# Low parts on VectorE, results read ahead of the weight sums, and the first down-weight sums moved one pair on

## What is computed

```
D_FF = -(-8 * D_MODEL // (3 * 256)) * 256
...
    h = h + m @ w_o
    hn = rms_norm(h, norm2_g)
    gate, up = jnp.split(hn @ w_gate_up, 2, axis=-1)
    return h + (jax.nn.silu(gate) * up) @ w_down
```

## Time and profile before

| | |
|---|---|
| three runs | 2266.13, 2267.99, 2269.9 us; median 2267.99 |
| profiled execution | 2270.73 us, span 2269.0 us |
| TensorE busy | 2179.5 us, 96% |
| VectorE, ScalarE, POOL busy | 1428.4 us (63%), 913.6 us (40%), 1024.8 us (45%) |
| mean granted clock of TensorE | 0.985 |
| the MLP's up and gate blocks | 1142.9 to 1592.7 us |

### The profile page before, as it was taken

The page is one execution under the profiler, slowest core; times in us unless marked ns, Lnnn a source line. Parts: engine busy times, 40 slices in busy tenths (PEclk is TensorE's granted clock), DMA queues, the critical chain, the costliest instruction groups (busy, mean ns, idle before and its releaser), DMA issues.

```text
span 2269.0 us, 29879 instructions
## 1 busy us (share of the span) xinstructions
PE 2179.5 (96%) x10752; PEld 1800.1 (79%) x10752; DVE 1428.4 (63%) x2788; ACT 913.6 (40%) x1625; POOL 1024.8 (45%) x580
## 2 busy tenths in 40 slices
PE   6999999999999989999979999999999999999998
PEld 5886688998888777778857888888888878888886
DVE  4248799999932366655597666565557746206944
ACT  5234522233224574433442323323445554226743
POOL 1265433455544233225556545556588723121063
PEclk8999999999999999999999999999999999999999
DMA  5112111111224213025623545444876321111131
GB/s 189 45 49 73 56 47 51 51 52 38 66 83 140 64 48 98 29 93 177 199 66 126 176 144 177 144 169 171 293 250 201 115 105 54 47 47 38 39 121 74
DMA packets 243829, 238.46 MB, mean 105 GB/s; under 512 B 10337, under 2 KB 186110, under 8 KB 243694
## 3 DMA queue, kind: packets, MB, share of 16 engines
q1 hardware_dynamic: 239536, 223.49, 30.4%
q10 hardware_dynamic: 4158, 13.16, 1.4%
HBM read 174.54 MB, written 61.15 MB: 104 GB/s over the span
## 4 chain that ended last, share of the span: by engine, by line
PE 76%; DVE 7%; issue 2%; ACT 2%; POOL 1%; ACTq 0%; DVEq 0%
PE ps L982 23%; PE ps L1269 17%; PE ps L1297 9%; PE ps L1343 9%; PE ps L1159 6%; PE ps L1564 4%; PE ps L1542 2%; PE ps L1191 1%; DVE logit L2402 1%; PE ps L1134 1%; PE ps L1177 1%; PE ps L1527 1%; DVE pt_lo L2421 1%; PE ps L1511 1%; PE ps L1501 0%
## 5 line engine op out<-in xcount | busy, mean ns | idle before, releaser
L3030 POOL TENSOR_TENSOR w_lo<-w_raw,w_hi 128x1024 fp32r<-128x1024 f32 (+1 forms) x129 | 295.2, 2289 | 760.6 <-ACT w_hi L1593 760.6
L982 PE MATMUL ps<-x_hi,w_hi 128*128 128x512 f32 (+2 forms) x960 | 360.9, 376 | 4.0 <-DVE c_rs L2319 3.3
L982 PE MATMUL ps<-x_lo,w_hi 128*128 128x512 f32 (+2 forms) x960 | 359.1, 374 | 0.0
L982 PE MATMUL ps<-x_hi,w_lo 128*128 128x512 f32 (+2 forms) x960 | 357.1, 372 | 0.0
L982 PEld LDWEIGHTS ps<-x_hi,w_hi 128*128 128x128 f32 x960 | 180.9, 188 | 39.7 <-issue 9.1
L982 PEld LDWEIGHTS ps<-x_hi,w_lo 128*128 128x128 f32 x960 | 181.2, 189 | 28.7
L982 PEld LDWEIGHTS ps<-x_lo,w_hi 128*128 128x128 f32 x960 | 180.7, 188 | 28.6 <-issue 0.2
L2377 DVE MATCH_REPLACE8 score<-best,score 128x400 f32<-128x400 f32 (+3 forms) x224 | 185.2, 829 | 0.0
L2373 DVE MAX8 best<-score 128x8 f32<-128x400 f32 (+3 forms) x224 | 181.2, 842 | 1.4
L1593 ACT CAST w_hi<-w_raw 128x1024 fp32r<-128x1024 f32 (+1 forms) x129 | 127.7, 990 | 103.0 <-PE ps L982 73.0
L1269 PE MATMUL ps<-x_hi,wr_hi 128*128 128x512 f32 x352 | 139.5, 396 | 3.1 <-DVE x_lo L2526 2.0
(11 more groups left out here) (473 smaller groups left out, 5453.3 us busy)
## 6 DMA issues: line engine op xcount, KB each, us to landing
w_raw<-in_w_in SPq DMA_DIRECT2D x74, 512.0 KB, 3.7
wdr<-as_scratch SPq DMA_DIRECT2D x77, 256.0 KB, 4.0
rawg<-in_w_gate_up SPq DMA_DIRECT2D x22, 512.0 KB, 3.9
rawu<-in_w_gate_up SPq DMA_DIRECT2D x22, 512.0 KB, 5.4
wdr<-in_w_down SPq DMA_DIRECT2D x22, 512.0 KB, 6.4
as_scratch<-ac SPq DMA_DIRECT2D x44, 256.0 KB, 3.7
wt_scratch<-wdr SPq DMA_DIRECT2D x33, 256.0 KB, 4.9
as_scratch<-a SPq DMA_DIRECT2D x33, 256.0 KB, 4.0
```

The source lines that it names most:

```text
L982: mm = pe.matmul(ps[:, b, 0:n], w[:, s, P * k:P * k + P], r[:, k, t0:t0 + n], start=k == 0 and i == 0, stop=k == kd - 1 and i == 2 and ext ...
L3030: pool.tensor_tensor(w_lo[:, p % 2, 0:n], w_raw[:, p % 2, 0:n], w_hi[:, p % 2, 0:n], ALU.subtract).then_inc(wlo_done, 1)
```

## The change

Four things change. VectorE makes all low parts of y = 16 to 27, the even ones too, which POOL made. The three first result reads of pair 0 come right behind them; `block_low(13)` follows, then the other reads of pairs 0 and 1, and only then `combined_weights(2)` and `block_low(15)`. ScalarE no longer waits for `combined_weights(n)` before it casts P1 and P2 of a pair n from 2 on (they are loaded weights). And POOL's `down_combined(0)` and `down_combined(1)` move from (2, 0) and (2, 6) of its loop over pairs and steps to (3, 0) and (3, 4).

```diff
--- before.py
+++ after.py
@@ -1867,7 +1867,7 @@
                 else:
                     n, prod = product_of(q)
                     act.wait_ge(raw_pair[n % 2], RAW_PAIR_0[n % 2] + 32 * (n // 2 + 1))
-                    if n >= 2 or prod not in ("P1", "P2"):
+                    if prod not in ("P1", "P2"):
                         act.wait_ge(tw_done, TW_DONE_0 + 4 * n + 4)
                 if q >= SLOTS:
                     act.wait_ge(blk_done, BLK_DONE_0 + q - SLOTS + 1)
@@ -2519,11 +2519,11 @@
                 dve.tensor_tensor(sr(1, s), wdr[:, s % 4, :], sr(0, s), ALU.subtract).then_inc(sl_even, 1)
 
             def x_low(y):
-                if y % 2 == 0:
-                    return
                 dve.wait_ge(xh_done, y + 1)
+                if y == 16:
+                    dve.wait_ge(*low_x(14))
                 prod, k = FIRST[y // 4], y % 4
-                dve.tensor_tensor(xb(1, prod, k), x_source(y), xb(0, prod, k), ALU.subtract).then_inc(xl_odd, 1)
+                dve.tensor_tensor(xb(1, prod, k), x_source(y), xb(0, prod, k), ALU.subtract).then_inc(xl_odd if y % 2 else xl_even, 1)
 
             def inverse(h):
                 c = slice(4 * h, 4 * h + 4)
@@ -2603,22 +2603,20 @@
                 dve.wait_ge(*low_x(8 + k))
                 dve.tensor_tensor(mix[:, 4 + k, half(1)], mix[:, 4 + k, half(1)], mix[:, k, half(1)], ALU.add).then_inc(s0_done, 1)
             block_low(9)
-            x_low(17)
-            x_low(19)
+            for k in range(16, 20):
+                x_low(k)
             for k in range(4):
                 dve.wait_ge(s0_done, S0_DONE_0 + 4 + k + 1)
                 dve.tensor_tensor(mix[:, k, half(1)], mix[:, 4 + k, half(1)], mix[:, k, half(0)], ALU.subtract).then_inc(s0_done, 1)
             block_low(11)
-            x_low(21)
-            x_low(23)
+            for k in range(20, 24):
+                x_low(k)
             for k in range(4):
                 dve.wait_ge(s0_done, S0_DONE_0 + 8 + k + 1)
                 dve.wait_ge(*low_x(4 + k))
                 dve.tensor_tensor(mix[:, 4 + k, half(0)], mix[:, 4 + k, half(0)], mix[:, k, half(1)], ALU.subtract).then_inc(s0_done, 1)
-            x_low(25)
-            x_low(27)
-            block_low(13)
-            combined_weights(2)
+            for k in range(24, 28):
+                x_low(k)
             for n in range(2):
                 a = a_st[0][n]
                 dve.wait_ge(r1_done, n + 1)
@@ -2629,9 +2627,11 @@
                 dve.tensor_tensor(g1[n][:, :], a[0][:, :], ps[:, bank_of(n, "P7"), :], ALU.add).then_inc(po_done, 1)
                 dve.wait_ge(po_done, po(n, 2))
                 dve.tensor_tensor(a[1][:, :], g1[n][:, :], ps[:, bank_of(n, "P5"), :], ALU.add).then_inc(po_done, 1)
+                if n == 0:
+                    block_low(13)
                 dve.tensor_tensor(g1[n][:, :], g1[n][:, :], ps[:, bank_of(n, "P4"), :], ALU.add).then_inc(po_done, 1)
-                if n == 0:
-                    block_low(15)
+            combined_weights(2)
+            block_low(15)
             for n in range(2):
                 a = a_st[0][n]
                 dve.wait_ge(blk_done, BLK_DONE_0 + 13 + n)
@@ -3231,13 +3231,7 @@
             x_low(12)
             x_low(14)
             block_low(10)
-            x_low(16)
-            x_low(18)
-            x_low(20)
-            x_low(22)
             block_low(12)
-            x_low(24)
-            x_low(26)
             block_low(14)
             block_low(16)
             for n in range(2):
@@ -3265,9 +3259,9 @@
                     block_low(7 * n + 6 + i)
                     if n == FC - 1 and i >= 1:
                         inner_low(i - 1)
-                    if (n, i) in ((2, 0), (2, 6)):
+                    if (n, i) in ((3, 0), (3, 4)):
                         pool.wait_ge(am_done, AM_DONE_0 + 4)
-                        down_combined(i // 6)
+                        down_combined(i // 4)
                     if i == 3 and n % 2 == 0 and n >= 4:
                         down_combined(n // 2)
                     if i == 5:
```

## The result

The changed kernel takes 2278.71 us (median of 5 runs, 2276.58 to 2285.77), the kernel before 2267.99 (5 runs, 2263.74 to 2270.45). The ratio is 1.0052, with a 95% interval from 1.004 to 1.0064: slower by some 11.8 us. The forecast was 7.4 us, with a range up to 2279.5; the ratio applied to the median of before gives 2279.8, just outside, though the median of its own five runs lies inside. The profiled execution of the changed kernel took 2280.36 us, its span is 2278.6.

A forecast was written before the change was run, and what follows sets the result against it. The prediction took TensorE, busy 96% of the span, as the bound, so only its idle time or clock matters. It summed -6.3 + 10.9 + 2.8 = +7.4 us on 2268.0, giving 2275.4 us, range 2269.5 to 2279.5.

The forecast's parts named there:

- the price of ScalarE's wait: Later pairs' P1 and P2: POOL's low part may hold VectorE 1.2 us in the weight sums; costed at nothing.
- The true wait of q12: 6.6 us stall at q12: waits for VectorE's queue (read of P5), not `wr_lo`; q12 would start 6.2 us earlier.
- one hold of 1.2: VectorE's queue before q12: POOL's q12 weights (1.2 us) fall among four low parts.
- 6.3 us earlier at q20: Pair 2's P3: q20 starts at 1212.1 instead of 1218.42; bounds 5.0 and 7.5 us.
- a slow clock at q12: Slow clock after q12's stall would be hidden by q20, since q18 and q20 wait for VectorE.
- 10.9 us later from q20 to q25: Moved sums delay SP's load of pair 4: q20's start to q25's takes 25.4 us, before 14.46; bounds 23.2 and 27.
- 2.8 us for the clock: After the stall before q25, TensorE works at its lower level and loses 2.8 us; bounds 1.7 and 3.5.
- cover of 1.5 us: Odd pairs: from L2701's end (starts 1270.00, takes 0.68) to P2's end at 1272.2, called the closest.
- a new short wait in each pair of odd number: Sign of being wrong: pairs of odd number show a new short TensorE wait each.
- The faster rival: Before q25: pair 4's load is not what is waited for; kernel takes 2261.1 us if the chain fits entirely; chance 0.08.
- waits of 1.5 to 2.5 us at q18 and q20: Sign of being right: q18 and q20 each wait 1.5 to 2.5 us for VectorE.

The follow-up runs named there:

- the best version: Kernel before plus new VectorE/POOL order, sums at (2, 4) and (3, 4), pair 4's load first, q12's low weights on VectorE, ScalarE's wait dropped for pair 2: 2262.23 us, ratio 0.9965.

## Why the prediction was right, and where it was not

The step that failed is the price of ScalarE's wait, put at nothing; the other terms came out within 1.1 us each.

- **The true wait of q12** (VectorE's read of P5, not the `wr_lo` in the row): right. With the reads ahead of the weight sums q12 started 7.3 us earlier. The forecast had 6.2: it put POOL's q12 weights into VectorE's queue as one hold of 1.2. In fact VectorE was not held at all, its four low parts took 2.49, and POOL stood. That extra 1.1 was gone again at `combined_weights(2)`, which waited 1.2 us for the load of pair 2, a wait that the forecast did not have.
- **6.3 us earlier at q20**: 5.2. L2707 ended 69.1 us after q0, just as forecast, but by luck: q18 started 1.3 us later than forecast, mainly since a weight sum was held (L2505, 1.64 us for 0.69), and the inner sums behind it took one hold instead of two. The forecast hid a slow clock at q12 behind later waits and had none at q18. L2707 ended at 1209.1, before q19 did, so the stretch of 3.3 us at the lower level behind q18's stall lay on the path of q20 and cost what was left.
- **10.9 us later from q20 to q25**: 10.6, each link within 0.3 us of its row. Three experiments show the cause: moving the sums alone makes a loss of 9.3 us, and moving them back or issuing the load first makes the changed kernel 10 to 11 us faster.
- **2.8 us for the clock**: 2.9. That it fits so well is luck: behind stalls of 10.2, 10.5 and 11.1 us at the same place in three other runs (ScalarE's wait back, the sums moved alone, q12's weights alone) the lower level lasted 4.9, 4.2 and 3.4 us, not 5.7.
- **ScalarE's wait, "so I cost it at nothing": the step that failed.** The mechanism was written down (POOL's low part falls into `combined_weights`), but its cover of 1.5 us was read from pair 5 and called the closest. In the kernel before, pair 9 has less. The read on VectorE, and the ScalarE operation that starts as P2 ends:

```profile
1348.68 0.68 DVE L2701 TENSOR_TENSOR a<-r1a,ps 128x512 f32<-128x512 f32 x1
```

```profile
1350.28 0.60 ACT L1900 ACTIVATE g0a<-ps 128x512 f32<-128x512 f32 x1 [0.81 <-PE ps L1269]
```

  From the end of the one to the start of the other is a cover of 0.9, less than the 1.1 that a hold costs. Pair 15 has 0.9 too and pair 19 has 1.2; pairs 7, 11, 13 and 17 have 1.7 to 2.0. All are some 0.3 too large if taken this way, since P7 starts 0.2 us before that ScalarE operation, and 0.15 us after a read that it waits for.

  What it cost: in the changed kernel TensorE stalls before P7 of pairs 9, 13, 15 and 19, 1.9 us by the profile's idle time. By the starts of the blocks (2.79 us for one that nothing stops) the blocks around these four places and one in pair 17 take 3.2 us more, and the clock behind q25 takes 2.7; that makes the +5.8 of the table. One hold is not the whole of it: in pair 13 the weight sums also start 1.0 us later against P7 than before, behind POOL's queue. The other runs agree. From q25 to the last block it takes 362.1 us in the two kernels without ScalarE's wait and without a long stall there, and 359.5 in the four that have the wait and no long stall. Giving the wait back took 3.4 us off the ratio, though with overlapping intervals. So this is most of the gap between +7.4 and +11.8. The prediction had named it as a sign of being wrong, a new short wait in each pair of odd number; it came in four of them.
- The edits one at a time, each on the kernel before, gave +9.3 (the sums), -1.8 (the new order, an interval that reaches no change) and +1.6 (the wait, not to be told from nothing). They sum to +9.1; the changed kernel's interval is +9.1 to +14.5. So they may simply add up, or cost a little more together; that is open.
- **The faster rival** (the load is not what is waited for): refuted by the 16.3 us for which VectorE waited for it. What it would have given, 2261.1, is near what the best version reached by other edits (2262.23).

The profile of the changed kernel also has a slow stretch from 1162.6 to 1166, 1.7 us of loss, behind a stall of 2.0 us that the kernel before has as well, without one. It cost nothing at q12, which waited for VectorE (1.61 us idle). Two more of the prediction's signs missed: it wanted waits of 1.5 to 2.5 us at q18 and q20, and q18 waited 3.4, q20 not at all.

## What to carry to other kernels

When work that fills another engine's gap is moved back, look first at what the in-order DMA queue waits for behind it: here four sums, 5.4 us together, held a load that the following weight sums needed, and cost 13.5 us. A wait that seems superfluous may be what keeps two engines off the same ports; its cover has to be read in every pair, not in one. And a gain at one stall has to be followed to the next place where engines meet before it is counted.

## What the runs showed of the hardware

VectorE and POOL don't always take turns. In most places an operation was held once by the other engine, 1.7 us for 0.68 and 1.29. But beside twelve operations of VectorE on two SBUF inputs, one operation of POOL took 7.7 us. The timeline of POOL, and of VectorE beside it:

```profile
1172.10 7.73 POOL L3193 TENSOR_TENSOR wr_lo<-rawu,wr_hi 128x512 fp32r<-128x512 f32 x1 [9.03 <-ACT wr_hi L1874]
```

```profile
1171.37 2.49 DVE L2526 TENSOR_TENSOR xl_P<-mix,xh_P 128x512 fp32r<-128x512 f32 x4
1173.78 2.49 DVE L2617 TENSOR_TENSOR mix<-mix 128x512 f32<-128x512 f32 x4
1176.18 2.49 DVE L2526 TENSOR_TENSOR xl_P<-mix,xh_P 128x512 fp32r<-128x512 f32 x4
1178.59 0.68 DVE L2625 TENSOR_TENSOR a<-r1a,ps 128x512 f32<-128x512 f32 x1
```

VectorE's twelve keep their 0.6 us from start to start, and POOL's ends at 1179.83, 1.24 after the first operation that reads PSUM starts, which is about its length alone. Ten of the twelve started while POOL's was under way. The Trainium skill ("SBUF — State Buffer", section "SBUF: two separate sides") says that whoever starts first gets the ports; the trace agrees that it is a lock, since the one side kept its full pace while the other stood, and adds that the engine that waits can miss its turn ten times over. Five more kernels with that order showed 7.70 to 7.73 us.

What decides it isn't shown. An unbroken run of VectorE isn't enough: in the kernel before, POOL met the same L2617, as unbroken, and had its turn at once. The four took 3.58 us for 2.49, so one was held, and POOL's two took 3.33:

```profile
1179.79 3.58 DVE L2617 TENSOR_TENSOR mix<-mix 128x512 f32<-128x512 f32 x4
```

```profile
1181.20 3.33 POOL L3204 TENSOR_TENSOR xl_P<-mix,xh_P 128x512 fp32r<-128x512 f32 x2 [2.48 <-ACT xh_P L1890]
```

What the clock does after a short stall can't be forecast from the stall: the same one of 2.0 us, before the second part of q6, was followed by a stretch of some 3.4 us at the lower level in 7 of 12 profiles, and by none in 5. The eight stalls of 5.0 to 11.1 us in this part were all followed by one, of 3.4 to 5.8 us.
